# Order of the softmax steps in the differential attention of a hybrid encoder layer

## The chip, the cores and the metric

The kernel runs on one core of a Trainium2 chip. A core has five engines that run side by side, each with its own in-order queue: TensorE (PE: matrix products and transposes into PSUM), VectorE (DVE), ScalarE (ACT), GpSimd (POOL) and SyncE (SP, which issues the DMAs). They wait for one another by semaphores. The metric is the device time of one execution in microseconds (us); lower is better.

## The reference

Two encoder layers over 528 positions (16 learned ones and 512 of the input), width 1024. In each layer one projection feeds four token mixers; their outputs are joined, projected (`w_out`) and added to the residual `h`, and a SwiGLU block follows. The change is in the third mixer, differential attention with 4 heads, each of which has two softmax maps:

```python
def attend(qb):
    p = softmax_probs(qb, k, scale).reshape(b, DIFF_HEADS, 2, qb.shape[1], t)
    amap = p[:, :, 0] - lam_full * p[:, :, 1]
    return jnp.einsum('bhqk,bkhd->bqhd', amap.astype(v.dtype), v)
o = sweep_query_blocks(attend, q)
o = rms_norm(o, out_g) * (1.0 - lambda_init)
```

## The kernel before

The kernel is written for each engine by hand: one function per engine, whose loops give the order of its queue, with semaphore waits between them. Nothing is scheduled by a planner in the stretch of this change. Dense products are made with each operand split in a lead and a rest part (fp32r), three products for each block of 128; ScalarE makes the lead of a weight slot (L1434) and GpSimd the rest (L584, `parts`).

Differential attention is done in 20 **units** (`DIFF_U`), unit u = 5 hp + i: head hp of 4, query tile i of 5 (four of 128 rows, the last of 16). In this text a unit's steps have these names:

- **Scores** (`score_pair`, L1213, TensorE): both score maps of the unit, into PSUM pairs 0 and 1. They may start once the unit before has been exponentiated.
- **Maxima** (`row_max`, L1825 and L1826, VectorE), one for each of the two maps.
- **Exponentials** (`softmax`, L1383, ScalarE), two, into `ebuf`.
- **Inverse sums** (`inverse_sums`, L1840 and L1841, VectorE), then **scaling** of the second map (`scaled_second`, L1394, ScalarE), then the **difference** of the two maps (`difference`, L1847, VectorE) into `mbuf`, which has two buffers.
- **Transposes** (`turn`, L1226 and L1228, TensorE) into one PSUM bank. They wait for the unit's difference and for the rests of the unit before, which free the bank.
- **Leads** (`turned_leads`, L1401, and L1403 for the tail at i = 3, ScalarE) and then **rests** (`turned_rests`, L1855, and L1859 for the tail, VectorE): they take the transposed map out of PSUM as a lead and a rest part.

When the five units of a head are done, **attend** (L800, `pb<-proj_r,v_parts`, 30 products) multiplies the turned map by the values; it waits for the last rests and for the **residual** of the dense group before (`residual`, L1767, VectorE), since both use one PSUM pair. ScalarE then copies the output out and squares it (`out_dif`, L1414 and L1342), TensorE sums the squares (`norm_sum`), ScalarE makes the reciprocal root (`rstd_dif`, L1358 and L1359) and VectorE applies it (`normed`, L1789, **the norm**), on which GpSimd splits the result in lead and rest (`mixed_split`, L610 and L612), followed by the rest part of the next weight slot (L584). Between these steps TensorE does pieces of the output projection (**dense pieces**, `beside`; L800 in layer 0, and L830 to L832 in layer 1): 12, 12, 12, 6 and 6 products in the units of head 0, and none, none, 18, 18 and 12 in the units of each later head in layer 0.

Of the kernel before, what the change touches and what calls it, by code (L numbers as in the profile page):

```python
# [97 lines left out]
DIFF_U = DIFF_H * NT  # L98
N_MAP = MLA_H + DIFF_H
N_EV = NT + 1  # L100
N_ATT_M = MLA_H * NT
# [57 lines left out]
def trunk(nc, x_t, w_stream, w_heads, params, consts, out):  # L159
    ctx = ExitStack()  # L160
    with ctx:
# [67 lines left out]
        def tile_of(buf, k, a=0, b=T, rows_=slice(0, P)):  # L229
            return buf[rows_, k * T + a:k * T + b]  # L230
# [92 lines left out]
        def turn_unit(u):  # L323

            return (u // NT, u % NT) if u < N_ATT_M else (MLA_H + (u - N_ATT_M) // NT, (u - N_ATT_M) % NT)
# [5 lines left out]
        def turned_blocks(tile0, i):  # L331

            a, w = TILES[i]
            n = NT - 1 if i < NT - 1 else NT
            return proj_r[:, tile0 * T:(tile0 + n) * T].rearrange("p (j t) -> p j t", t=T)[:, :, a:a + w]
# [7 lines left out]
        def turned_tail(tile0):  # L343

            return proj_r[0:TILES[-1][1], (tile0 + NT - 1) * T:(tile0 + NT - 1) * T + 512]
# [14 lines left out]
        def dense_part(u):  # L360

            hp, i = u // NT, u % NT
            if hp == 0:
                return ((0, 2), (2, 4), (4, 6), (6, 7), (7, 8))[i]
            return (None, None, (0, 3), (3, 6), (6, 8))[i]
# [430 lines left out]
        def _(pe):  # L796
# [7 lines left out]
            def norm_sum(l, s0, n, p, rows_=slice(0, P), ones="ones"):  # L804

                for k in range(n):
                    pe.wait_ge(sq_ready.sem, sq_ready.at(l, s0 + k + 1))
                    product(p, C(ones, rows_), sq[rows_, (s0 + k) % 2, :], k == 0, k == n - 1).then_inc(sq_used.sem, 1)
# [36 lines left out]
            def beside(l, g, j, operand, chunks):  # L845

                if chunks[j][0] == 0 and chunks[j][1] > 0:
                    pe.wait_ge(evac.sem, evac.at(l, g))
                split_product(l, g, *chunks[j], operand)
# [265 lines left out]
            for l in range(DEPTH):  # L1115
# [89 lines left out]
                def score_pair(u):  # L1205

                    hp, i = u // NT, u % NT
                    pe.wait_ge(p_ready.sem, p_ready.at(l, N_ATT_M + 2 * u))
                    a, w = TILES[i]
                    for b in range(2):  # L1210
                        for m in range(2):
                            r = slice(64 * m, 64 * m + 64)
                            last = nc.tensor.matmul(pb[0:w, 2 * m + b, 0:HALF], tile_of(proj, DQ + hp, a, a + w, r),  # L1213
                                                    tile_of(proj, DK + hp, b * HALF, (b + 1) * HALF, r), start=True, stop=True)
                            if b == 1:
                                last.then_inc(s_ps.sem, 1)
# [40 lines left out]
                for n in range(N_ATT_M):  # L1257
                    hd, i = n // NT, n % NT
# [23 lines left out]
                pe.wait_ge(evac.sem, evac.at(l, G_OUT1 + 3))  # L1282
                norm_sum(l, SQ_A, 4, 3)
                pe.wait_ge(tr_evac.sem, tr_evac.at(l, TR_DV + NT))
                for u in range(DIFF_U):
                    hp, i = u // NT, u % NT
                    if u + 1 < DIFF_U:
                        score_pair(u + 1)
                    if i == 0 and hp:
                        pe.wait_ge(evac.sem, evac.at(l, G_OUT1 + 3 + hp))  # L1290
                        attend(MLA_H + hp - 1)
                    turn(N_ATT_M + u)
                    if i == 1 and hp:
                        pe.wait_ge(o_evac.sem, o_evac.at(l, MLA_H + hp))
                        norm_sum(l, SQ_O + hp - 1, 1, 3)
                    if dense_part(u):
                        pe.wait_ge(rs_ready.sem, rs_ready.at(l, RS_OD + hp))
                        beside(l, G_OUT1 + 3 + hp, 0, mixed_parts, (dense_part(u),))
                pe.wait_ge(evac.sem, evac.at(l, G_OUT2 - 1))
                attend(N_MAP - 1)  # L1300
                beside(l, G_OUT2 - 1, 0, mixed_parts, ((0, KD),))
# [29 lines left out]
        def _(act):  # L1331
# [64 lines left out]
            def turned_leads(l, u):  # L1396

                m, i = turn_unit(u)
                act.wait_ge(t_ps.sem, t_ps.at(l, u + 1))
                act.wait_ge(tails_zero.sem, tails_zero.at(l, 1))  # L1400
                nc.scalar.activation(turned_blocks(PT_LEAD, i), turned_sums(i), ACT.Copy).then_inc(pt_lead.sem, 1)  # L1401
                if i == NT - 2:
                    nc.scalar.activation(turned_tail(PT_LEAD), tail_sums(), ACT.Copy).then_inc(pt_lead.sem, 1)  # L1403
# [151 lines left out]
            for l in range(DEPTH):  # L1555
# [93 lines left out]
                for n in range(N_ATT_M):  # L1649
                    hd, i = n // NT, n % NT  # L1650
# [29 lines left out]
                rsqrt(l, SQ_A + 4, 3, 512, rstd2)  # L1680
                for u in range(DIFF_U):
                    hp, i = u // NT, u % NT
                    if i or hp == 0:
                        turned_leads(l, N_ATT_M + u)
                    if u + 1 < DIFF_U:
                        softmax(l, N_ATT_M + 2 * u + 2)
                        softmax(l, N_ATT_M + 2 * u + 3)
                        scaled_second(l, u + 1)
                    if i == 0 and hp:
                        out_dif(l, hp - 1)  # L1690
                        turned_leads(l, N_ATT_M + u)
                    if i == 0:
                        lead(l, S_OUT1 + 4 + hp)
                    if i == 1 and hp:
                        rstd_dif(l, hp - 1)
# [29 lines left out]
        def _(dve):  # L1725
# [37 lines left out]
            def residual(l, g, k):  # L1763

                dve.wait_ge(w_used.sem, w_used.at(l, slot_end(g)))
                now = of_group(l, g, h[:, k, :])
                nc.vector.tensor_tensor(now, now, group_sum(l, g), ALU.add).then_inc(evac.sem, 1)  # L1767
# [54 lines left out]
            def row_max(l, n):  # L1822
                dve.wait_ge(s_ps.sem, s_ps.at(l, n + 1))
                dve.wait_ge(p_ready.sem, p_ready.at(l, max(n - 1, 0)))
                link(nc.vector.tensor_reduce(rowmax[:, n % 2:n % 2 + 1], pair(n % 2), AX.XY, ALU.max))  # L1825
                nc.vector.tensor_scalar(negmax[:, n % 2:n % 2 + 1], rowmax[:, n % 2:n % 2 + 1], -scale_of(n), None,  # L1826
                                        ALU.mult).then_inc(max_ready.sem, 1)
# [22 lines left out]
            def turned_rests(l, u):  # L1850

                m, i = turn_unit(u)
                e = m * N_EV + i
                dve.wait_ge(pt_lead.sem, pt_lead.at(l, e + 1 + (i == NT - 1)))
                nc.vector.tensor_tensor(turned_blocks(PT_REST, i), turned_sums(i), turned_blocks(PT_LEAD, i).bitcast(FP32),  # L1855
                                        ALU.subtract).then_inc(pt_rest.sem, 1)
                if i == NT - 2:
                    dve.wait_ge(pt_lead.sem, pt_lead.at(l, e + 2))
                    nc.vector.tensor_tensor(turned_tail(PT_REST), tail_sums(), turned_tail(PT_LEAD).bitcast(FP32),  # L1859
                                            ALU.subtract).then_inc(pt_rest.sem, 1)  # L1860
# [223 lines left out]
            for l in range(DEPTH):  # L2084
# [15 lines left out]
                for g in range(G_SSD):  # L2100
# [16 lines left out]
                    if g == MISC + 2:  # L2117
# [4 lines left out]
                        u, ln = ebuf[d24, 0, :], ebuf[d24, 1, :]  # L2122
# [75 lines left out]
                for n in range(N_ATT_M):  # L2198
                    hd, i = n // NT, n % NT
# [18 lines left out]
                for i in range(NT):  # L2218
# [3 lines left out]
                    nc.vector.tensor_tensor(parts_of[:, :, 1, :], pb[0:w, 4 + (TR_DV + i) % 2, 0:512].rearrange("p (h v) -> p h v", h=DIFF_H),  # L2222
                                            parts_of[:, :, 0, :].bitcast(FP32), ALU.subtract).then_inc(tr_evac.sem, 1)
                residual(l, G_OUT1 + 2, 2)
                for u in range(DIFF_U):
                    hp, i = u // NT, u % NT
                    if u + 1 < DIFF_U:
                        row_max(l, N_ATT_M + 2 * u + 2)
                        row_max(l, N_ATT_M + 2 * u + 3)
                    if i or hp == 0:  # L2230
                        turned_rests(l, N_ATT_M + u)
                    if u + 1 < DIFF_U:
                        inverse_sums(l, u + 1)
                        difference(l, u + 1)
                    if i == 0 and hp:
                        turned_rests(l, N_ATT_M + u)
                    if u == 0:
                        dve.wait_ge(rs_ready.sem, rs_ready.at(l, RS_OA + 1))
                        for f in range(4):
                            normed(l, tile_of(mix_f, 12 + f), par_at(l, "mla_out_g", f), count=(f == 3))  # L2240
                    if i == 2 and hp:
                        dve.wait_ge(rs_ready.sem, rs_ready.at(l, RS_OD + hp))
                        normed(l, tile_of(proj, DV + hp - 1), gain_d[:, :])
                    if i == NT - 1:
                        residual(l, G_OUT1 + 3 + hp, 3 + hp)
# [195 lines left out]
```

## Time and profile before

| | |
|---|---|
| median of 3 runs | 2339.93 us (2337.79 to 2340.47) |
| the profiled execution, its own time | 2344.09 us |
| its span, first to last instruction | 2342.3 us |
| busy PE, DVE, ACT, POOL | 2118.8, 1089.6, 854.8, 997.9 us |
| mean granted TensorE clock | 0.972 |
| differential attention, layer 0 (first scores of unit 1 to the last attend) | 620.63 to 735.36 us |
| the same in layer 1 | 1798.08 to 1912.35 us |

TensorE is busy for 90% of the span, so it is the engine that sets the time of the kernel as a whole; but that is a mean over stages, and in the two stretches of the last two lines it is busy for 71% only. The table's last two lines are starts of rows of the trace, which give the place of the stretches. A row of a timeline reads: start, duration, engine, line of the kernel, operation, out<-in, shapes, count; in brackets the idle time of that engine just before, and what ended it.

### The profile page before, as it was taken

The numbers are of one execution on the slowest core, as the hardware profiler recorded it, in microseconds if no ns is written. First come the engines' busy times: TensorE is split into PE (matmuls) and PEld (weight loads), VectorE is DVE, ScalarE is ACT, GpSimd is POOL, SyncE is SP. The second block draws the span as 40 slices with busy tenths as digits, with TensorE's granted clock in tenths as the row PEclk, the third lists the DMA queues.
The fourth block names the chain that finished last, engine by engine and source line by source line (L and its number), as shares of the span: only waits on it lengthen the run. The fifth ranks groups of instructions, "written<-read, shape, count | busy, mean of one in ns | idle before, by whom it ended". The sixth has DMA issues, their size and how long they took to land.

```text
span 2342.3 us, 33441 instructions
## 1 busy us (share of the span) xinstructions
PE 2118.8 (90%) x13634; PEld 1822.7 (78%) x13634; DVE 1089.6 (47%) x1699; ACT 854.8 (36%) x1400; POOL 997.9 (43%) x592
## 2 busy tenths in 40 slices
PE   7999998878778999999989999988777779999999
PEld 7888886556667999999988888865555557888887
DVE  8642354555565644441066322545555657444400
ACT  3322343566554222222223222435665543222221
POOL 4365333664312444444433554336642124444444
PEclk9999999899999999999999999998999899999999
DMA  4211111000001222223322211110000012232333
GB/s 155 64 56 62 47 55 54 10 1 19 19 19 46 83 91 90 91 90 99 99 73 64 64 55 55 46 63 10 1 19 19 19 35 92 91 99 91 98 102 114
DMA packets 40040, 143.85 MB, mean 61 GB/s; under 512 B 4433, under 2 KB 4561, under 8 KB 39761
## 3 DMA queue, kind: packets, MB, share of 16 engines
q1 hardware_dynamic: 39888, 141.72, 18.9%
q8 instruction: 109, 1.79, 0.3%
q14 instruction: 43, 0.34, 0.0%
HBM read 139.60 MB, written 2.10 MB: 60 GB/s over the span
## 4 chain that ended last, share of the span: by engine, by line
PE 71%; DVE 14%; ACT 8%; issue 4%; POOL 1%; DMA 1%; ACTq 0%; SPq 0%; DVEq 0%; POOLq 0%
PE pb L800 44%; PE pb L831 6%; PE pb L830 6%; PE pb L832 6%; ACT ebuf L1383 3%; DVE kh L1779 2%; PE pb L1226 2%; DVE rowmax L1825 1%; ACT ebuf L1394 1%; DVE proj L1761 1%; DVE mbuf L1847 1%; ACT rstd L1358 1%; PE pb L1082 1%; ACT rstd L1359 1%; PE pb L930 1%
## 5 line engine op out<-in xcount | busy, mean ns | idle before, releaser
L584 POOL TENSOR_TENSOR parts<-raw,parts 128x1024 fp32r<-128x1024 f32 x248 | 604.8, 2439 | 844.4 <-ACT parts L1434 844.2
L800 PE MATMUL pb<-mix,parts 128*128 128x264 f32 x4608 | 671.0, 294 | 40.3 <-POOL parts L584 17.1
L800 PEld LDWEIGHTS pb<-mix,parts 128*128 128x128 f32 x4608 | 609.5, 194 | 65.6 <-issue 28.1
L1434 ACT ACTIVATE parts<-raw 128x1024 fp32r<-128x1024 f32 x248 | 262.4, 1058 | 826.7 <-PE pb L800 525.1
L800 PE MATMUL pb<-proj_r,parts 128*128 128x264 f32 x3104 | 429.1, 286 | 0.5 <-POOL parts L584 0.5
L800 PEld LDWEIGHTS pb<-proj_r,parts 128*128 128x128 f32 x3104 | 401.2, 189 | 0.8 <-issue 0.7
L830 PE MATMUL pb<-proj_r,parts 128*128 128x512 f32 x528 | 207.4, 393 | 0.8 <-DVE mbuf L1761 0.8
L832 PE MATMUL pb<-proj_r,parts 128*128 128x512 f32 x528 | 207.7, 393 | 0.0
L831 PE MATMUL pb<-proj_r,parts 128*128 128x512 f32 x496 | 198.0, 399 | 0.0
L1767 DVE TENSOR_TENSOR h<-h,pb 128x528 f32<-128x528 f32 (+1 forms) x48 | 33.3, 694 | 272.7 <-PE pb L800 139.1
L1383 ACT ACTIVATE ebuf<-pb,negmax 128x528 f32<-128x528 f32 x160 | 110.9, 696 | 56.0 <-DVE negmax L1826 55.5
L1761 DVE TENSOR_TENSOR mbuf<-pb,rstd 128x528 f32<-128x528 f32 (+1 forms) x44 | 30.8, 700 | 214.8 <-PE pb L800 110.5
L1761 DVE TENSOR_TENSOR proj<-pb,rstd 128x528 f32<-128x528 f32 x80 | 56.5, 706 | 156.3 <-PE pb L800 143.3
L1825 DVE TENSOR_REDUCE rowmax<-pb 128x1 f32<-128x528 f32 x160 | 112.6, 704 | 31.5 <-PE pb L800 20.4
L800 PE MATMUL pb<-sq,con 128*128 128x264 f32 (+1 forms) x328 | 91.2, 409 | 31.4 <-ACT sq L1629 22.1
L830 PEld LDWEIGHTS pb<-proj_r,parts 128*128 128x128 f32 x528 | 99.2, 188 | 24.9 <-DVE mbuf L1761 1.2
L832 PEld LDWEIGHTS pb<-proj_r,parts 128*128 128x128 f32 x528 | 99.3, 188 | 22.4
L2272 DVE CAST proj_r<-ebuf 128x528 fp32r<-128x528 f32 x44 | 110.9, 2521 | 1.5
L831 PEld LDWEIGHTS pb<-proj_r,parts 128*128 128x128 f32 x496 | 94.7, 191 | 20.8
L800 PE MATMUL pb<-proj_r,v_parts 128*128 128x264 f32 x560 | 81.2, 305 | 25.2 <-ACT rstd L1359 16.2
L800 PEld LDWEIGHTS pb<-proj_r,v_parts 128*128 128x128 f32 x560 | 76.1, 206 | 35.3 <-ACT rstd L1359 21.2
L800 PE MATMUL pb<-proj,w_head 128*112 128x264 f32 (+1 forms) x320 | 85.2, 417 | 15.8 <-DMA w_head<-w_heads 9.8
(273 smaller groups left out, 2877.7 us busy)
## 6 DMA issues: line engine op xcount, KB each, us to landing
raw<-w_stream SPq DMA_DIRECT2D x250, 512.0 KB, 3.5
w_head<-w_heads SPq DMA_DIRECT2D x8, 512.0 KB, 4.8
h<-x_t SPq DMA_DIRECT2D x8, 264.0 KB, 6.6
out_t<-h SPq DMA_DIRECT2D x8, 256.0 KB, 4.9
con<-consts SPq DMA_DIRECT2D x1, 1652.5 KB, 10.3
par<-params SPq DMA_DIRECT2D x1, 340.0 KB, 4.4
con<-consts SPq DMA_DIRECT2D x1, 128.0 KB, 6.8
```

Of the source, the lines that this page charges most:

```text
L584: nc.gpsimd.tensor_tensor(parts[:, n % PARTS, 1, :], w, parts[:, n % PARTS, 0, :].bitcast(FP32), ALU.subtract).then_inc(split.sem, 1)
L800: last = nc.tensor.matmul(pb[rows_, 2 * p + a, 0:HALF], lhs_t, rhs[:, a * HALF:(a + 1) * HALF], start=start, stop=stop)
L830: nc.tensor.matmul(o, w_lead, lead[:, kept(l, g)], start=(k == 0), stop=False)
L831: nc.tensor.matmul(o, w_lead, rest[:, kept(l, g)], start=False, stop=False)
L832: last = nc.tensor.matmul(o, w_rest, lead[:, kept(l, g)], start=False, stop=(k == k_all - 1))
L1226: nc.tensor.transpose(pb[:, TURN, j * step:j * step + P], src[:, j * P:(j + 1) * P], C("ident"))
L1383: nc.scalar.activation(halves(ebuf[:, b, :]), pair(b), ACT.Exp, scale=scale_of(n), bias=negmax[:, b:b + 1], accum_out=sums[:, n % 4:n % 4 ...
L1434: nc.scalar.activation(parts[:, n % PARTS, 0, :], raw[:, r % RAW, :], ACT.Copy).then_inc(lead_ready.sem, 1)
L1761: nc.vector.tensor_tensor(of_group(l, g, dst), group_sum(l, g), of_group(l, g, rstd[:, :]), ALU.mult).then_inc(evac.sem, 1)
L1779: ins = nc.vector.scalar_tensor_tensor(out=acc[:, a:b], in0=src[:, a + s:b + s], scalar=par_at(l, "conv_w", f * TAPS + mid + s), in1=acc[: ...
L1825: link(nc.vector.tensor_reduce(rowmax[:, n % 2:n % 2 + 1], pair(n % 2), AX.XY, ALU.max))
L2272: link(nc.vector.tensor_copy(lead, prod))
```

## The change

In the loop over the units the steps are written in another order, on three engines. On ScalarE the leads of a unit now always stand behind the next unit's exponentials and scaling, as they did before at i = 0 only. On VectorE the rests now always stand behind the next unit's difference, and the maxima are made for the unit after the next, behind the rests. On TensorE the scores of unit u+2 are written at the end of unit u instead of at the start of unit u+1.

```diff
@@ TensorE
+                score_pair(1)
                 for u in range(DIFF_U):
                     hp, i = u // NT, u % NT
-                    if u + 1 < DIFF_U:
-                        score_pair(u + 1)
                     if i == 0 and hp:
...
                         beside(l, G_OUT1 + 3 + hp, 0, mixed_parts, (dense_part(u),))
+                    if u + 2 < DIFF_U:
+                        score_pair(u + 2)
@@ ScalarE
                     hp, i = u // NT, u % NT
-                    if i or hp == 0:
-                        turned_leads(l, N_ATT_M + u)
                     if u + 1 < DIFF_U:
                         softmax(l, N_ATT_M + 2 * u + 2)
                         softmax(l, N_ATT_M + 2 * u + 3)
                         scaled_second(l, u + 1)
                     if i == 0 and hp:
                         out_dif(l, hp - 1)
-                        turned_leads(l, N_ATT_M + u)
+                    turned_leads(l, N_ATT_M + u)
@@ VectorE
+                row_max(l, N_ATT_M + 2)
+                row_max(l, N_ATT_M + 3)
                 for u in range(DIFF_U):
                     hp, i = u // NT, u % NT
                     if u + 1 < DIFF_U:
-                        row_max(l, N_ATT_M + 2 * u + 2)
-                        row_max(l, N_ATT_M + 2 * u + 3)
-                    if i or hp == 0:
-                        turned_rests(l, N_ATT_M + u)
-                    if u + 1 < DIFF_U:
                         inverse_sums(l, u + 1)
                         difference(l, u + 1)
-                    if i == 0 and hp:
-                        turned_rests(l, N_ATT_M + u)
+                    turned_rests(l, N_ATT_M + u)
+                    if u + 2 < DIFF_U:
+                        row_max(l, N_ATT_M + 2 * u + 4)
+                        row_max(l, N_ATT_M + 2 * u + 5)
                     if u == 0:
...
```

The queue of TensorE has the same 3507 rows in the same order in both kernels: the scores of unit u+2 at the end of one turn of the loop and at the start of the next are the same place. So the change is one of ScalarE and VectorE alone. All lines behind the change stand one or two lower in the new kernel.

ScalarE before, head 1, from the leads of unit 6 on:

```order
L1401 ACTIVATE proj_r<-pb 128x4x128
L1383 ACTIVATE ebuf,sums<-pb,negmax 128x528 x2
L1394 ACTIVATE ebuf<-ebuf,rsum 128x528
L1358 ACTIVATE rstd<-pb,eps 128x528
L1359 ACTIVATE rstd<-rstd 128x528
L1401 ACTIVATE proj_r<-pb 128x4x128
L1383 ACTIVATE ebuf,sums<-pb,negmax 128x528 x2
L1394 ACTIVATE ebuf<-ebuf,rsum 128x528
```

and now, from the exponentials of unit 7 on:

```order
L1384 ACTIVATE ebuf,sums<-pb,negmax 128x528 x2
L1395 ACTIVATE ebuf<-ebuf,rsum 128x528
L1402 ACTIVATE proj_r<-pb 128x4x128
L1359 ACTIVATE rstd<-pb,eps 128x528
L1360 ACTIVATE rstd<-rstd 128x528
L1384 ACTIVATE ebuf,sums<-pb,negmax 128x528 x2
L1395 ACTIVATE ebuf<-ebuf,rsum 128x528
L1402 ACTIVATE proj_r<-pb 128x4x128
```

The leads (L1401, now L1402) have moved from ahead of the next unit's exponentials to behind its scaling.

VectorE before, from the maxima of unit 8 through the norm (L1789) to the maxima of unit 9:

```order
L1825 TENSOR_REDUCE rowmax<-pb 128x1
L1826 TENSOR_SCALAR negmax<-rowmax 128x1
L1855 TENSOR_TENSOR proj_r<-pb,proj_r 128x4x128
L1840 RECIPROCAL rsum<-sums 128x2
L1841 TENSOR_TENSOR rsum<-rsum,neg_lam 128x1
L1847 SCALAR_TENSOR_TENSOR mbuf<-ebuf,rsum 128x528
L1789 SCALAR_TENSOR_TENSOR proj<-proj,gain_d,rstd 128x528
L1825 TENSOR_REDUCE rowmax<-pb 128x1
L1826 TENSOR_SCALAR negmax<-rowmax 128x1
```

and now, from the inverse sums of unit 8 on:

```order
L1839 RECIPROCAL rsum<-sums 128x2
L1840 TENSOR_TENSOR rsum<-rsum,neg_lam 128x1
L1846 SCALAR_TENSOR_TENSOR mbuf<-ebuf,rsum 128x528
L1854 TENSOR_TENSOR proj_r<-pb,proj_r 128x4x128
L1824 TENSOR_REDUCE rowmax<-pb 128x1
L1825 TENSOR_SCALAR negmax<-rowmax 128x1
L1824 TENSOR_REDUCE rowmax<-pb 128x1
L1825 TENSOR_SCALAR negmax<-rowmax 128x1
L1788 SCALAR_TENSOR_TENSOR proj<-proj,gain_d,rstd 128x528
```

The rests (L1855, now L1854) stand behind the difference, the maxima behind the rests, and the norm behind the maxima.

VectorE before, at the end of a head, from the last unit's rests (L1855, 128x5x16) over the residual (L1767) to the maxima of the next head's second unit:

```order
L1855 TENSOR_TENSOR proj_r<-pb,proj_r 128x5x16
L1840 RECIPROCAL rsum<-sums 128x2
L1841 TENSOR_TENSOR rsum<-rsum,neg_lam 128x1
L1847 SCALAR_TENSOR_TENSOR mbuf<-ebuf,rsum 128x528
L1767 TENSOR_TENSOR h<-h,pb 128x528
L1825 TENSOR_REDUCE rowmax<-pb 128x1
L1826 TENSOR_SCALAR negmax<-rowmax 128x1
```

and now:

```order
L1846 SCALAR_TENSOR_TENSOR mbuf<-ebuf,rsum 128x528
L1854 TENSOR_TENSOR proj_r<-pb,proj_r 128x5x16
L1824 TENSOR_REDUCE rowmax<-pb 128x1
L1825 TENSOR_SCALAR negmax<-rowmax 128x1
L1824 TENSOR_REDUCE rowmax<-pb 128x1
L1825 TENSOR_SCALAR negmax<-rowmax 128x1
L1766 TENSOR_TENSOR h<-h,pb 128x528
```

The residual, for which attend waits, now has the last rests and two maxima ahead of it as well as the difference.

## Rows read from the trace of the kernel before

**Rows 1.** Busy time in head 0 of layer 0, by engine (windows view)
```profile
core 0: us, PE busy (x) PEld busy (x) DVE busy (x) ACT busy (x) POOL busy (x), PEclk, DMA share, GB/s
620.63:649.93 29.30, 17.74 (x122) 13.56 (x121) 20.62 (x47) 16.08 (x34) 13.66 (x9) 0.94 0.07 19
```
**Rows 2.** Waits of TensorE, 616 to 740 us: us in total, times, longest
```profile
PE pb L1226 <- DVE mbuf L1847: 16.5, 12, 3.6
PE pb L1213 <- ACT ebuf L1383: 10.4, 9, 2.9
```
**Rows 3.** Timeline of TensorE, layer 0, head 1: transposes of units 6, 7, 9, scores
```profile
658.07 0.63 PE L1226 MATMUL pb<-con,mbuf 128*128 128x128 f32 x4 [1.04 <-DVE proj_r L1855]
662.82 0.65 PE L1226 MATMUL pb<-con,mbuf 128*128 128x128 f32 x4 [0.81 <-DVE mbuf L1847]
665.71 1.07 PE L1213 MATMUL pb<-proj 64*16 64x264 f32 x8
674.16 1.03 PE L1226 MATMUL pb<-con,mbuf 128*128 128x128 f32 x4 [2.13 <-DVE mbuf L1847]
```
**Rows 4.** Timeline of VectorE, one unit: maxima, inverse sum, difference, rests, maxima
```profile
649.80 0.70 DVE L1825 TENSOR_REDUCE rowmax<-pb 128x1 f32<-128x528 f32 x1
652.36 0.17 DVE L1840 RECIPROCAL rsum<-sums 128x2 f32<-128x2 f32 x1 [0.86 <-ACT ebuf L1383]
653.52 0.77 DVE L1847 SCALAR_TENSOR_TENSOR mbuf<-ebuf,rsum 128x528 f32<-128x528 f32 x1 [0.80 <-ACT ebuf L1394]
657.23 0.69 DVE L1855 TENSOR_TENSOR proj_r<-pb,proj_r 128x512 fp32r<-128x512 f32 x1 [2.94 <-ACT proj_r L1401]
657.84 0.70 DVE L1825 TENSOR_REDUCE rowmax<-pb 128x1 f32<-128x528 f32 x1
659.47 0.69 DVE L1855 TENSOR_TENSOR proj_r<-pb,proj_r 128x512 fp32r<-128x512 f32 x1
666.78 0.77 DVE L1847 SCALAR_TENSOR_TENSOR mbuf<-ebuf,rsum 128x528 f32<-128x528 f32 x1 [0.80 <-ACT ebuf L1394]
```
**Rows 5.** Timeline of VectorE: rests and tail at i = 3, the next inverse sum
```profile
669.77 0.68 DVE L1855 TENSOR_TENSOR proj_r<-pb,proj_r 128x512 fp32r<-128x512 f32 x1
670.96 0.14 DVE L1840 RECIPROCAL rsum<-sums 128x2 f32<-128x2 f32 x1
```
**Rows 6.** End of head 0, layer 0: last transposes, last rests, residual, attend
```profile
644.90 0.65 PE L1226 MATMUL pb<-con,mbuf 128*128 128x128 f32 x4 [0.81 <-DVE mbuf L1847]
646.39 0.23 DVE L1855 TENSOR_TENSOR proj_r<-pb,proj_r 128x80 fp32r<-128x80 f32 x1
649.18 0.70 DVE L1767 TENSOR_TENSOR h<-h,pb 128x528 f32<-128x528 f32 x1
649.93 5.46 PE L800 MATMUL pb<-proj_r,v_parts 128*128 128x264 f32 x30 [1.42 <-DVE h L1767]
```
**Rows 7.** VectorE and GpSimd side by side, from the norm of head 0
```profile
667.46 0.76 DVE L1789 SCALAR_TENSOR_TENSOR proj<-proj,gain_d,rstd 128x528 f32<-128x528 f32 x1
668.31 1.53 POOL L610 TENSOR_SCALAR mix<-proj 128x528 fp32r<-128x528 f32 x1 [25.07 <-DVE proj L1789]
669.93 1.31 POOL L612 TENSOR_TENSOR proj_r<-proj,mix 128x528 fp32r<-128x528 f32 x1
671.20 2.35 POOL L584 TENSOR_TENSOR parts<-raw,parts 128x1024 fp32r<-128x1024 f32 x1
672.10 2.01 DVE L1847 SCALAR_TENSOR_TENSOR mbuf<-ebuf,rsum 128x528 f32<-128x528 f32 x1 [0.80 <-ACT ebuf L1394]
```
**Rows 8.** Head 0, layer 0: first maxima, the four norms, GpSimd's run
```profile
621.82 0.71 DVE L1825 TENSOR_REDUCE rowmax<-pb 128x1 f32<-128x528 f32 x1 [5.18 <-PE pb L1213]
626.37 2.80 DVE L1789 SCALAR_TENSOR_TENSOR mix_f<-mix_f,par,rstd 128x528 f32<-128x528 f32 x4
629.25 1.53 POOL L610 TENSOR_SCALAR mix<-mix_f 128x528 fp32r<-128x528 f32 x1 [20.67 <-DVE mix_f L1789]
640.90 2.35 POOL L584 TENSOR_TENSOR parts<-raw,parts 128x1024 fp32r<-128x1024 f32 x1
```

## The prediction

> **What bounds the kernel now.** I read the page first for the share of each engine, then the busy times of the two stretches in which differential attention runs, then TensorE's waits there, and last the timelines, since the change is an order of instructions. TensorE sets the time of the kernel, but in head 0 of this stage it is busy for 17.74 of 29.30 us, and no other engine for more than 20.62 [rows 1]. So no engine is full: the stage is a chain that goes from engine to engine. TensorE's waits say which. Of the 114.7 us of the stretch in layer 0, 16.5 are waits of the transposes for the difference of the maps, and 10.4 are waits of the scores for the exponentials [rows 2]. Both point at the softmax of the next unit.
>
> In a plain unit before, the chain closes through the transposes: transposes of unit u, its leads on ScalarE, the exponentials of u+1 behind them, inverse sum, scaling, difference of u+1, transposes of u+1. One turn is 4.75 us (658.07 to 662.82) [rows 3]. In it TensorE has its own work, transposes and 18 dense products, 2.89 us from 662.82 to 665.71, and 1.07 of scores [rows 3]. Together that is 4.0, so at most some 0.8 us of a turn is open to a better order.
>
> **The change, part by part.** *TensorE.* Its queue has the same rows in the same order, so this edit costs and gives nothing. "Two units ahead" was already so. SP's queue and GpSimd's are untouched, and the order of the weight leads on ScalarE too.
>
> *The new chain.* ScalarE now exponentiates u+1 ahead of the leads of u, so the transposes and leads leave the chain. But VectorE has its whole work for a unit in one row, and it makes the maxima of u+2 only behind the rests of u. What ScalarE may exponentiate next hangs on those maxima. The new turn is therefore: maxima of u+1, exponentials, inverse sum, scaling, difference of u+1, rests of u, maxima of u+2. Each step has a row. From the first of the two maxima to the inverse sum, 649.80 to 652.36, 2.56; from there to the difference, 653.52, 1.16; from a difference to the next VectorE instruction, 666.78 to 667.46, 0.68 [rows 4, 7]; from rests to maxima, 657.23 to 657.84, 0.61 [rows 4]. The sum is 5.01 us. The leads are not what is late in it: the scaling and then the leads end before VectorE has got through the difference. The scores are there in time at full clock: they start 2.89 behind the transposes, which follow the rests by 0.84 (657.23 to 658.07) [rows 3, 4], so the maxima find them some 0.7 us early. Transposes come one per turn, so a plain unit goes from 4.75 to 5.01: it takes 0.26 more. The cover that the old order had (the maxima stood under the transposes and leads) is what is given up.
>
> *Units 6 to 9 of each later head.* Before, from the transposes of unit 6 to those of unit 9 it is 16.09 us (658.07 to 674.16) [rows 3]: two plain turns, and a third of 6.56 with a tail and a stall in it. The stall is the difference that took 2.01 instead of 0.77, 1.24 us, while GpSimd's subtraction of 671.20 to 673.55 ran [rows 4, 7]. Now: three turns of 5.01 are 15.03, since the tail of unit 8 falls behind the rests for which unit 9's transposes wait. Whether the stall remains is a matter of place. The norm now stands behind the maxima of unit 9, so it starts 2.56 - 1.63 = 0.93 us before the inverse sum (two maxima are 1.63, 657.84 to 659.47 [rows 4]) and the difference 2.09 behind its start. GpSimd's first subtraction begins 2.47 behind the norm's start (667.46 to 669.93) and its second ends 6.09 behind (to 673.55) [rows 7]. The difference gets in 0.4 us ahead of the first, and the next unit's two-input instructions come at some 6.7, behind the second. So I take the stall as gone: 15.03 - 16.09 = -1.06 for each of three heads.
>
> The Trainium skill, "SBUF — State Buffer", section "🔬 SBUF: two separate sides", says that VectorE and GpSimd share a port pair as an exclusive lock, held for a whole instruction, and that a VectorE instruction with two SBUF inputs is of the kind that needs it. The trace agrees: the difference ran on past the end of GpSimd's subtraction, and the rests, which read PSUM and took 0.68 under the other subtraction at 669.77 [rows 5, 7], did not. By that rule a shift of 0.4 us turns the gain into a loss, which is rival B.
>
> *The end of a head.* Attend waits for the residual, and the residual now has more ahead of it. Before, from the last unit's transposes to attend is 5.03 us (644.90 to 649.93) [rows 6]. Now, from the rests of unit 3 on: tail 1.19 (669.77 to 670.96) [rows 5], maxima and exponentials of the next unit 2.56, inverse sum to difference 1.16, difference 0.68, last rests 0.23 (646.39) [rows 6], two more maxima 1.63, residual to attend 0.75 (649.18 to 649.93) [rows 6]. That is 8.20 from the rests of unit 3, and the transposes of unit 4 stand 0.84 behind those, so 7.36: +2.33. Behind attend the order is that of before (leads at i = 0 were already behind the scaling), so nothing changes up to unit 6. The last head has no maxima left to put ahead of the residual: 0.
>
> *Head 0.* From its first maxima (621.82 [rows 8]) to the rests of unit 0 is 2.56 + 1.16 + 0.68 = 4.40, the next maxima follow 0.61 behind and end at 628.46. The four norms (2.80 [rows 8]) now stand there, over the exponentials of unit 2, to 631.26; the rests of unit 1 follow at 631.26 + 1.16 + 0.68 = 633.10. Two turns more bring the rests of unit 3 to 643.1, and 8.20 more attend to 651.3, against 649.93: +1.4. Stalls come on top. GpSimd's run of four splits and a weight part started 2.88 behind the norms (629.25) and ended at 643.25 [rows 8]; it shifts by the 2.1 us of the norms, and the new instants of the inverse sums and the difference fall in up to three of its subtractions, by my walk 3.0 us in all. Since fractions of a microsecond decide each, I take 2.0, between none and 3.0. Head 0: +3.4.
>
> **The sum.** One layer: head 0 +3.4; heads 1 and 2 each -1.06 + 2.33 = +1.27, together +2.5; head 3 -1.06. That is +4.9, and both layers have the same order: +9.8 us. The profiled execution (2344.09: the span of 2342.3 and 1.8 around it) would go to 2353.9; it stood 4.2 over the median of the runs, so against the median of 2339.93 I say 2349.7.
>
> The bounds: with no stall in head 0, 2.9 a layer, +5.8 and 2345.7. With all of them, +11.8 and 2351.7. TensorE's lowered clock is a second term. Unit 9's transposes took 1.03 instead of 0.65, and attend 5.46 [rows 3, 6]; in such a stretch the scores come later than the 0.7 us that the new chain has in hand. From double durations (2.89 more) this would cost up to 2 us each; two or three in a layer, if they fall so, are +4 to +8 for both layers. I leave it out of the centre and keep it in the range.
>
> **The rivals.** *A. The intended gain.* If VectorE kept pace with TensorE, a unit would take 4.0 us. Units 6 to 9 would go to 12, -4.1 for three heads, -1.5 in head 0, +2.3 for three heads' ends: -7 a layer, 2326. It decides where VectorE's serial row is under 4.0; the rows add up to 5.01. A weaker form (the end of a head cheaper, fewer lowered-clock stretches) stays between 2326 and 2335. Against it: attend's place behind the residual is in the order itself. For it: the waits for the difference, 16.5 us [rows 2], are real, and they are what the edit goes for. 12 in 100.
>
> *B. The stall moves and grows.* If the difference of unit 9 is 0.4 us later than worked out, it meets both subtractions in a row and waits 3.3 us, in three heads and two layers: +20, so 2369. If only half of them fall so, 2359. The margin is small, but it is made of VectorE's own row and a fixed lag of GpSimd, which move together. 12 in 100, with 3 of them at the full price.
>
> *C. It cancels.* If the residual's delay is half covered (its dense piece ends late anyway at a lowered clock, as in the head of rows 3) and head 0 has no new stalls, what units 6 to 9 give, -6.4 in all, meets half of the ends, +4.7, and head 0's +2.8: +1.1, so 2341. 13 in 100.
>
> **How the numbers follow.** My forecast has 63 in 100, with its own range 2345 to 2357. From no change one can tell 0.2%, that is 4.7 us. Slower is my case and B, 75 in 100; the same C, 13; faster A, 12. The range reaches down into C and up into B: 2339 to 2361.
>
> **What would show it.** In the profile after: transposes of plain units 5.0 us apart, with the wait before them named for the rests (L1854) and no longer for the difference; ScalarE's leads with no wait; maxima 0.6 behind the rests. From the last transposes of a head to attend 7.4 us, with the residual as releaser; in the last head 3 to 5. Unit 9's difference 0.77 long, and long ones, if any, in head 0. Heads 1 and 2 each 1.3 longer, head 3 one shorter. I am wrong if a plain unit is under 4.75, if attend is not held by the residual, or if the difference of unit 9 still runs for 2 us or more.

## The result and the profile after

The changed kernel is slower: median 2358.49 us (2355.15 to 2360.26, 4 runs) against 2340.2 us for the kernel before (4 runs), ratio 1.0072, 95% interval 1.0054 to 1.0090. The profiled execution took 2360.26 us, its span 2358.4: 16.1 more than before. All of it lies in differential attention. From the first scores of unit 1 to the last attend, layer 0 went from 114.7 to 121.5 us and layer 1 from 114.3 to 124.0, +16.5 together.

The two largest waits of TensorE in layer 0 of the changed kernel (waiting line, releaser, us in total, times, longest):

```profile
PE pb L1226 <- DVE proj_r L1854: 25.3, 16, 3.7
PE pb L800 <- DVE h L1766: 10.9, 5, 3.2
```

The transposes no longer wait for the difference, as in [rows 2], but for the rests; and attend's wait for the residual is now the second largest. Both were foretold; how long each is the timelines show. VectorE in head 1 of the changed kernel, one plain unit, then unit 9's product of the inverse sum with `neg_lam` (L1840) and its difference (start, duration, line, operation):

```profile
668.63 0.70 DVE L1824 TENSOR_REDUCE rowmax<-pb 128x1 f32<-128x528 f32 x1
671.20 0.17 DVE L1839 RECIPROCAL rsum<-sums 128x2 f32<-128x2 f32 x1 [0.86 <-ACT ebuf L1384]
672.36 0.77 DVE L1846 SCALAR_TENSOR_TENSOR mbuf<-ebuf,rsum 128x528 f32<-128x528 f32 x1 [0.80 <-ACT ebuf L1395]
673.04 0.68 DVE L1854 TENSOR_TENSOR proj_r<-pb,proj_r 128x512 fp32r<-128x512 f32 x1
673.64 0.69 DVE L1824 TENSOR_REDUCE rowmax<-pb 128x1 f32<-128x528 f32 x1
676.41 0.34 DVE L1840 TENSOR_TENSOR rsum<-rsum,neg_lam 128x1 f32<-128x1 f32 x1
677.55 0.77 DVE L1846 SCALAR_TENSOR_TENSOR mbuf<-ebuf,rsum 128x528 f32<-128x528 f32 x1 [0.80 <-ACT ebuf L1395]
```

From maxima to maxima it is 5.01 us (668.63 to 673.64), and the steps are those of [rows 4] within 0.01: 2.57, 1.16, 0.68, 0.60. The difference of unit 9 takes 0.77 instead of the 2.01 of [rows 7]. What TensorE does in the same head (transposes of units 6 to 9, then attend):

```profile
663.85 0.63 PE L1226 MATMUL pb<-con,mbuf 128*128 128x128 f32 x4 [1.04 <-DVE proj_r L1854]
668.86 0.63 PE L1226 MATMUL pb<-con,mbuf 128*128 128x128 f32 x4 [1.49 <-DVE proj_r L1854]
673.87 0.63 PE L1226 MATMUL pb<-con,mbuf 128*128 128x128 f32 x4 [1.08 <-DVE proj_r L1854]
679.07 0.63 PE L1226 MATMUL pb<-con,mbuf 128*128 128x128 f32 x4 [1.20 <-DVE proj_r L1854]
686.36 5.45 PE L800 MATMUL pb<-proj_r,v_parts 128*128 128x264 f32 x30 [3.19 <-DVE h L1766]
```

Units 6 to 9 take 15.22 us (16.09 in [rows 3]), and the last transposes to attend 7.29 (5.03 in head 0 before, [rows 6]). New in this head is the duration of attend itself, 5.45 us. In the kernel before it was:

```profile
679.68 3.92 PE L800 MATMUL pb<-proj_r,v_parts 128*128 128x264 f32 x30 [0.64 <-DVE h L1767]
```

The windows view of the changed kernel, for the stretch ahead of attend and for attend itself (columns as in [rows 1]):

```profile
682.01:686.36 4.35, 1.16 (x9) 0.69 (x9) 3.39 (x9) 2.28 (x6) 0.00 (x0) 1.00 0.39 121
686.36:691.65 5.29, 5.29 (x31) 5.29 (x31) 1.09 (x3) 0.90 (x3) 0.00 (x0) 0.68 0.00 0
```

TensorE works for 1.16 of 4.35 us, then runs attend at a granted clock of 0.68 on average, a mix of 1.2 and 2.4 GHz; in the 15.7 us behind it the granted clock is 1.00 again. Before, of the six attends of heads 0 to 2 in both layers, two took about 5.5 us and four 3.9, 26.6 us in all. Now all six take 5.3 to 6.6, 34.3 us in all: +7.7. (The attends of the last head, which lie behind the end of the two stretches, took 5.6 and 5.9 us before and take 3.9 and 6.1 now.)

### The profile page after: what moved, and what is told of

It is laid out like the page before. It is cut to its first block, busy times and chain, and to the rows that moved or that the text cites. A ratio compares the mean times of both kernels' runs of the same rounds, so it can differ in the third digit from the quotient of the medians.

```text
span 2358.4 us, 33441 instructions
## 1 busy us (share of the span) xinstructions
PE 2121.2 (90%) x13634; PEld 1824.6 (77%) x13634; DVE 1086.5 (46%) x1699; ACT 858.0 (36%) x1400; POOL 1001.5 (42%) x592
## 4 chain that ended last, share of the span: by engine, by line
PE 70%; DVE 16%; ACT 8%; issue 4%; POOL 1%; DMA 1%; SPq 0%; ACTq 0%; DVEq 0%; POOLq 0%
PE pb L800 44%; PE pb L830 6%; PE pb L831 6%; PE pb L832 6%; DVE rowmax L1824 3%; ACT ebuf L1384 2%; DVE kh L1778 2%; DVE proj_r L1854 1%; PE pb L1226 1%; DVE proj L1760 1%; ACT ebuf L1395 1%; ACT rstd L1359 1%; PE pb L1082 1%; ACT rstd L1360 1%; PE pb L930 1%
## 5 line engine op out<-in xcount | busy, mean ns | idle before, releaser
L800 PE MATMUL pb<-proj_r,v_parts 128*128 128x264 f32 x560 | 87.4, 321 | 37.4 <-DVE h L1766 21.2
L800 PEld LDWEIGHTS pb<-proj_r,v_parts 128*128 128x128 f32 x560 | 82.3, 222 | 47.4 <-DVE h L1766 25.6
L610 POOL TENSOR_SCALAR mix<-proj 128x528 fp32r<-128x528 f32 x22 | 34.7, 1579 | 160.8 <-DVE proj L1788 160.1
```

The lines of the kernel that those rows point to most:

```text
L610: nc.gpsimd.tensor_scalar(lead, mixed_source(k), 1.0, None, ALU.mult).then_inc(mixed_lead.sem, 1)
L800: last = nc.tensor.matmul(pb[rows_, 2 * p + a, 0:HALF], lhs_t, rhs[:, a * HALF:(a + 1) * HALF], start=start, stop=stop)
```

## The experiments

Each ratio is that of a kernel to the kernel before, measured side by side on one chip. Where two of these ratios are compared with each other, both intervals count.

**The residual ahead of the maxima (e1_res_first).**

```diff
                     turned_rests(l, N_ATT_M + u)
+                    if i == NT - 1:
+                        residual(l, G_OUT1 + 3 + hp, 3 + hp)
                     if u + 2 < DIFF_U:
                         row_max(l, N_ATT_M + 2 * u + 4)
                         row_max(l, N_ATT_M + 2 * u + 5)
...
-                    if i == NT - 1:
-                        residual(l, G_OUT1 + 3 + hp, 3 + hp)
```

> The changed kernel, with the residual of the dense group put ahead of the two maxima at the end of a head, and nothing else. Theory (the row of VectorE sets the pace): from the last transposes of a head to attend it takes the 1.63 us of two maxima less, in three heads of two layers, -9.8 us, so about 2348.7; plain units stay at 5.01 us. Rival (TensorE's lowered clock in attend is brought on by the idle time ahead of it, 3.2 us in the changed kernel): the idle time falls to 1.6 us and attend goes back from 5.4 to 3.9 us in most heads, up to -9 more, so 2340. Rival (the residual is held by its dense piece and not by the maxima): no change, 2358.

Ratio 0.9999 (0.9987 to 1.0011): the whole loss is gone, 17 us of it. The row of VectorE alone asked for 9.8 of them, the reading with the clock for up to 9 more. In the trace of this kernel, the last transposes of head 1 and the attend behind them:

```profile
675.18 0.63 PE L1226 MATMUL pb<-con,mbuf 128*128 128x128 f32 x4 [1.18 <-DVE proj_r L1854]
680.85 3.89 PE L800 MATMUL pb<-proj_r,v_parts 128*128 128x264 f32 x30 [1.56 <-DVE h L1766]
```

From transposes to attend it is 5.67 instead of 7.29 us: the 1.63 of two maxima, 9.7 us in six places. Attend's wait is 1.56 instead of 3.19, and five of the six attends run at 3.9 us, 25.4 us in all in place of 34.3. So the residual's place is confirmed as its own term, and the rest, some 7 us, comes with the clock. The third reading, that the dense piece holds the residual, falls.

**VectorE's order alone (e2_vector_only).** ScalarE's part of the diff taken back. (ScalarE's part alone can't be run: leads behind the next scaling, with rests ahead of the next inverse sums, wait for each other.)

```diff
+                    if i or hp == 0:
+                        turned_leads(l, N_ATT_M + u)
                     if u + 1 < DIFF_U:
                         softmax(l, N_ATT_M + 2 * u + 2)
...
                     if i == 0 and hp:
                         out_dif(l, hp - 1)
-                    turned_leads(l, N_ATT_M + u)
+                        turned_leads(l, N_ATT_M + u)
```

> VectorE's order of the changed kernel with ScalarE's order of the kernel before (leads ahead of the next exponentials). Theory (one chain through all engines): transposes, leads 0.80, exponentials 0.50 + 0.67, inverse sum 0.83, difference 1.16, rests 0.68, transposes 0.84 make a turn of 5.5 us, against 4.75 before and 5.01 in the changed kernel, and the end of a head is as long as in the changed kernel: some 13 us a layer over the kernel before, about 2367. Rival (ScalarE's new order is what costs): it comes out at the time of the kernel before or up to 5 us over it.

Ratio 1.0154 (1.0129 to 1.0179), +36 us where 27 were expected. A turn is 5.45 us, as the chain says:

```profile
698.61 0.63 PE L1226 MATMUL pb<-con,mbuf 128*128 128x128 f32 x4 [1.04 <-DVE proj_r L1856]
704.07 0.63 PE L1226 MATMUL pb<-con,mbuf 128*128 128x128 f32 x4 [1.50 <-DVE proj_r L1856]
```

So VectorE's order is what costs; ScalarE's part of the change gives some of it back (5.45 to 5.01 a turn). Of the 9 us over my expectation 6.8 can be put down to attends at the lowered clock, by one trace: its six take 33.4 us in place of 26.6.

**Work in place of idling (e3_fill, e9_before_fill).** In the changed kernel five extra products, in the kernel before two:

```diff
                     if i == 0 and hp:
+                        pe.wait_ge(pt_rest.sem, pt_rest.at(l, (MLA_H + hp - 1) * N_EV + NT))
+                        for _ in range(5):
+                            nc.tensor.matmul(pb[:, TAIL, 0:HALF], C("ones"), C("cos_d")[:, 0:HALF], start=True, stop=True)
                         pe.wait_ge(evac.sem, evac.at(l, G_OUT1 + 3 + hp))
```

> The changed kernel, with five extra products (128x264, into the unused tail bank, results never read) on TensorE ahead of attend's wait in heads 1 to 3, so that it works through 2.6 of the 3.2 us for which it stood idle. Theory clock (the idle time ahead of attend brings the lowered clock): attend goes from 5.4 back to 3.9 us in most heads, -6 to -9 us in all, 2350 to 2352. Rival (the clock is lowered by what was done long before, or at fixed times): attend's mean length stays at 5.4 or grows, and the time stays within 2 us of 2358.

> The kernel before with two extra products of 128x264 on TensorE ahead of attend's wait in heads 1 to 3 (results never read), 1.0 of the 1.4 us that it idled there. Theory clock: of the three attends a layer that this reaches, one took 5.5 us in the kernel before; it goes to 3.9, -3 us in two layers, ratio 0.997 to 0.9985. The filled forms of both kernels (this one, and the changed kernel with five extra products, ratio 1.0027) then differ by what the order of the steps costs without the clock's share: by the prediction's terms 9.8 us, 0.42% of the time. Rival (the clock's share in the change is small, the chain costs all 17 us): this run comes out 15 us or more under the filled changed kernel, at 0.996 or less.

The changed kernel with the extra products: ratio 1.0027 (1.0016 to 1.0038), so useless work took 10 us off (6 to 15 with both intervals; 6 to 9 were expected). Its windows for the same two stretches as above:

```profile
686.11:690.46 4.35, 3.58 (x19) 2.51 (x19) 3.39 (x9) 2.28 (x6) 0.00 (x0) 1.00 0.37 121
690.46:694.21 3.75, 3.75 (x31) 3.75 (x31) 1.09 (x3) 0.90 (x3) 0.00 (x0) 1.00 0.02 4
```

The stretch ahead of attend is as long as before, 4.35 us, and attend runs at 2.4 GHz throughout. All six attends are at 3.9 to 4.0, 10.7 us less than in the changed kernel. That attend runs slowly because TensorE does little ahead of it is shown: only that was changed, and all 18 attends behind extra products in the three kernels that have them (e3, e9, e7) took 3.9 to 4.0 us. The Trainium skill, "TensorE: Matmul & The Clock Gate", section "🔬 Part 1: The HAM clock gate (the "warmup" mystery)", calls the low rate the default which activity releases; by that rule the trace agrees, 0.68 becoming 1.00.

The kernel before with extra products came out at 0.9997 (0.9987 to 1.0007). Its six attends took 23.7 us instead of 26.6, but no gain can be measured, where 0.997 to 0.9985 was expected; in its trace four groups of transposes in the later heads still took 1.04 to 1.12 us instead of 0.66, so the lowered clock was not gone from them. The filled forms of both kernels differ by 0.30%, some 7 us; with both intervals 3.5 to 10.5. That is what the order costs without the clock's share in attend, and my 9.8 lies in it; the rival of 15 us or more does not. The agreement is partly luck. In the two traces the stretches differ by 10.0 us, but 9.4 of it is in head 0, where the prediction has 6.8 (the five products outlast attend's shorter wait there, by 1.2 us in both layers), and 0.6 in heads 1 to 3, where it has 3.0.

**GpSimd's two-input instructions (e5_one_input, e6_before_one_input).** In both kernels those of this stage become one-input instructions, which copy the source. The subtraction is left out, so these two kernels don't compute the reference; only their times are used.

```diff
-                nc.gpsimd.tensor_tensor(parts[:, n % PARTS, 1, :], w, parts[:, n % PARTS, 0, :].bitcast(FP32),
-                                        ALU.subtract).then_inc(split.sem, 1)
+                if S_OUT1 + 4 <= s < S_OUT2:
+                    nc.gpsimd.tensor_scalar(parts[:, n % PARTS, 1, :], w, 1.0, None, ALU.mult).then_inc(split.sem, 1)
+                else:
+                    nc.gpsimd.tensor_tensor(parts[:, n % PARTS, 1, :], w, parts[:, n % PARTS, 0, :].bitcast(FP32),
+                                            ALU.subtract).then_inc(split.sem, 1)
...
-                nc.gpsimd.tensor_tensor(other, mixed_source(k), lead.bitcast(FP32), ALU.subtract).then_inc(mixed.sem, 1)
+                if k < KD:
+                    nc.gpsimd.tensor_tensor(other, mixed_source(k), lead.bitcast(FP32), ALU.subtract).then_inc(mixed.sem, 1)
+                else:
+                    nc.gpsimd.tensor_scalar(other, mixed_source(k), 1.0, None, ALU.mult).then_inc(mixed.sem, 1)
```

> The changed kernel, in which GpSimd makes the rest parts of the mixed rows 8 to 14 and of the weight slots of the stretch (four a layer) by one-input instructions (a copy of the source in place of source minus lead, so these rest parts are not the reference's). Theory (VectorE's two-input instructions wait behind GpSimd's two-input subtractions): the waits of head 0 in the changed kernel's trace, 0.45 + 0.68 + 0.81 + 1.28 = 3.2 us, and 0.18 in each later head go, 3.7 us a layer, -7.5 us: ratio to the kernel before about 1.004, 2351 us. The difference and the product with neg_lam then always take 0.77 and 0.16 us. Rival (they are long for another reason, such as PSUM or a DMA): their lengths and the time stay, 2358.

> The kernel before, with the same one-input instructions on GpSimd (the same rest parts left wrong). Theory: the 1.24 us stall in each of three heads and 0.7 us in head 0 go, 4.4 to 5.2 us a layer, -9 to -10 us, 2331. With the run on the changed kernel this prices the term 'the stall is gone': the difference between both kernels without any stall should be 11 to 12 us worse for the change where lowered clocks are alike. Rival: no change, 2340.

The kernel before gains as expected, 0.9959 (0.9943 to 0.9975), 9.6 us. The changed kernel comes to 1.0064 (1.0041 to 1.0087): 2 us under its own ratio, which the intervals don't separate from none. The 3.7 us a layer were expected to go entirely. By the trace 2.6 of them went in layer 0 and 2.0 in layer 1, and head 0 became 1.8 to 1.9 us shorter in each. What stays shows in the changed kernel, where VectorE's product at 676.41 (above, 0.34 long where it is 0.16 elsewhere) meets GpSimd's one-input instruction:

```profile
676.11 1.53 POOL L610 TENSOR_SCALAR mix<-proj 128x528 fp32r<-128x528 f32 x1 [29.17 <-DVE proj L1788]
677.73 1.75 POOL L612 TENSOR_TENSOR proj_r<-proj,mix 128x528 fp32r<-128x528 f32 x1
```

The product ends at 676.75, 0.64 us behind GpSimd's start. In the traces of the changed kernel, e4, e5, e6 and e8 there are 38 such products, which begin up to 0.31 us behind the start of a one-input instruction of this shape, and every one ends 0.63 to 0.66 behind that start, while a difference that begins later, 0.85 us behind such a start at 639.64 in the changed kernel, keeps its 0.77 us. So a one-input instruction on GpSimd also holds VectorE's two-input product up, for its first 0.6 of 1.5 us; the prediction took the hold to be for a whole instruction and of two-input ones only. That is part of why the expectation for this run was too high, and it is the 0.18 us by which the third turn (5.20) is over 5.01. The second row shows how near rival B was: unit 9's difference began at 677.55, 0.18 us ahead of the first subtraction, where the prediction counted on 0.4.

**A third order (e4_between), with the norm in its old place (e8_between_norm2), and filled (e7_between_fill).** If VectorE's row sets the pace, an order that puts its rests into a wait that it has anyway should be faster:

```diff
@@ ScalarE
                         softmax(l, N_ATT_M + 2 * u + 3)
+                    if i or hp == 0:
+                        turned_leads(l, N_ATT_M + u)
+                    if u + 1 < DIFF_U:
                         scaled_second(l, u + 1)
                     if i == 0 and hp:
                         out_dif(l, hp - 1)
-                    turned_leads(l, N_ATT_M + u)
+                        turned_leads(l, N_ATT_M + u)
...
@@ VectorE
                         inverse_sums(l, u + 1)
+                    if i or hp == 0:
+                        turned_rests(l, N_ATT_M + u)
+                    if u + 1 < DIFF_U:
                         difference(l, u + 1)
-                    turned_rests(l, N_ATT_M + u)
+                    if i == 0 and hp:
+                        turned_rests(l, N_ATT_M + u)
+                    if i == NT - 1:
+                        residual(l, G_OUT1 + 3 + hp, 3 + hp)
...
-                    if i == 2 and hp:
+                    if i == 3 and hp:
                         dve.wait_ge(rs_ready.sem, rs_ready.at(l, RS_OD + hp))
                         normed(l, tile_of(proj, DV + hp - 1), gain_d[:, :])
-                    if i == NT - 1:
-                        residual(l, G_OUT1 + 3 + hp, 3 + hp)
```

At i = 0 of the later heads ScalarE's leads stay behind `out_dif`. The residual stands ahead of the maxima here too, as in e1.

> A third order. ScalarE: exponentials of u+1, leads of u, scaling of u+1. VectorE: inverse sums of u+1, rests of u, difference of u+1, then the residual, then the maxima of u+2; the norm one unit later (i = 3). At i = 0 as in the changed kernel. Theory (the row of VectorE sets the pace): the rests stand under the scaling instead of behind the difference, so a turn is maxima 1.63, exponentials and inverse sum 0.93 and 0.83, leads and rests under the scaling, 1.35 to the difference, 0.68: about 4.5 us against 4.75 before; the end of a head is shorter by 1.6 us than in the changed kernel; unit 9's difference escapes GpSimd's subtractions. Together some 7 to 9 us a layer under the kernel before: 2322 to 2327. Rival (VectorE's order makes no difference, only ScalarE's leads do): about 2340.

> The third order with the norm left at i = 2 as in both kernels. Theory (GpSimd's subtractions start 2.5 us behind the norm): the shorter turn of 4.4 us puts the second inverse sum or difference behind the norm into the second subtraction again, 1 to 1.5 us in three heads of two layers, so 2330 to 2334, between the third order (2324.7) and the kernel before. Rival (the place of the norm is of no account): 2325.

> The third order (exponentials, leads, scaling) with three extra products of 128x264 on TensorE ahead of attend's wait in heads 1 to 3, results never read; 1.5 of the 1.6 us that it idled there. Theory clock (work in place of idling keeps the clock up): the four attends that took 5.45 us go back to 3.92, -6 us, 2319. Rival (the clock is lowered by something else): the count of slow attends stays, time 2325, or a little more where the extra products end late.

The third order gives 0.9925 (0.9904 to 0.9947), as expected, 17.6 us under the kernel before and 34 under the changed one. By e1 half of the 34 belongs to the residual's place. VectorE in the third order:

```profile
662.36 0.70 DVE L1827 TENSOR_REDUCE rowmax<-pb 128x1 f32<-128x528 f32 x1
664.93 0.17 DVE L1842 RECIPROCAL rsum<-sums 128x2 f32<-128x2 f32 x1 [0.86 <-ACT ebuf L1384]
665.41 0.69 DVE L1857 TENSOR_TENSOR proj_r<-pb,proj_r 128x512 fp32r<-128x512 f32 x1
666.09 0.77 DVE L1849 SCALAR_TENSOR_TENSOR mbuf<-ebuf,rsum 128x528 f32<-128x528 f32 x1
666.77 0.70 DVE L1827 TENSOR_REDUCE rowmax<-pb 128x1 f32<-128x528 f32 x1
```

From inverse sum to difference it is still 1.16 us, but now the rests stand in it, where VectorE waited for the scaling. The turn is 4.41 us. The norm's old place costs nothing that can be measured: 0.9923 (0.9901 to 0.9944), although unit 9's difference then takes 1.68 us. The stall came as expected, the loss of 5 us or more did not. By the traces four of six attends ran slow with the new place and one with the old, which gives back most of what the stall takes; that is an account after the fact. With three extra products the third order is the fastest kernel of this study, 0.9878 (0.9857 to 0.9899), median 2317.05 us; all its attends take 3.9 to 4.0. The gain over the third order is 11 us, 4 to 18 with both intervals; the slow attends had cost 6 there by my count, which lies in it. The windows view of its head 2:

```profile
676.12:701.58 25.46, 21.26 (x153) 16.90 (x153) 18.19 (x44) 17.34 (x36) 5.65 (x4) 1.00 0.06 22
```

A head is 25.46 us long there, at a granted clock of 1.00; in the changed kernel it was 30.6.

## Why the prediction was right, and where it was not

The direction and its mechanism were right: 2349.7 was forecast in 2339 to 2361, and 2358.5 was measured. The size was half: +9.8 against +18.3 by the medians, +16.5 in the two stretches. The measured time is over the 2345 to 2357 of my own case; it lies in the whole range only because that was stretched for rival B, whose 2359 was met without its mechanism. That is luck. Of the signs that I named, the turn, the releasers, 7.4 us to attend and the length of unit 9's difference came as said, the lengths of the heads did not.

- *TensorE's part changes nothing.* Right by its queue, which is the same.
- *A turn of 5.01 us in place of 4.75.* Right to 0.01. e2 (5.45) and e4 (4.41) confirm the chain from both sides, each order having its own sum.
- *Units 6 to 9: -1.06.* Measured 15.22 against 16.09, -0.87, in the head of the rows. The stall is gone, as foretold; the 0.18 us is GpSimd's one-input instruction, which I had taken to be harmless. Over all six heads it is -1.08 on average, since two of them took 17.42 and 16.66 before (one with a stall of 2.00 us instead of 1.24, both with transposes at a lowered clock). Rival B, the stall that grows, did not occur, but 0.18 us of margin was all that was left.
- *The end of a head: +2.33.* Measured 7.29 - 5.03 = +2.26; over all six heads 7.3 against 5.0 to 5.6, +2.02 on average. e1 shows that most of it, 1.62, is the residual's place. The last head's end, set at 0, became 0.6 us shorter.
- *Head 0: +3.4.* Measured +4.6 and +3.9. The stalls that I walked through to 3.0 us and then set at 2.0 all occurred. In layer 0 three under subtractions make 0.68 + 0.81 + 1.28 = 2.8 us, and a fourth, under a one-input instruction, adds 0.45. The walk should have been trusted.
- *"TensorE's lowered clock is a second term ... I leave it out of the centre and keep it in the range."* This term failed. I priced it through late scores (+4 to +8, where two or three a layer at up to 2 us make up to 8 to 12) and gave it 0 in the sum. In fact it sits in attend: six attends took 34.3 us in place of 26.6, +7.7, and e3 took 10.7 off them by filling the wait ahead. Every step that I had made longer was a wait of TensorE, and at the end of a head it grew from at most 1.4 us to 2.4 to 3.2. I had the row that shows the price, attend at 5.46 [rows 6], and counted only late scores from it.
- *The terms together.* By the traces the 9.8 us became 16.5 so: +1.7 in head 0, -1.3 at the ends of heads 1 and 2, -1.2 at those of the last heads, and +7.7 in attend. The misses other than attend's nearly offset each other.
- *Rivals A and C.* A fell on VectorE's sum; what it hoped for is what e4 then did, by making that sum 4.41. C asked for a half covered residual, and it was not covered at all.

Heads 1 to 3 changed by +0.9, +1.6, -0.3 in layer 0 and +1.3, +3.5, +1.1 in layer 1. Two layers with one order differ mostly by what the clock did, so only their sum is held against the prediction.

## What to carry to other kernels

Where no engine is full, write down for each engine the row of its steps in one turn, with the steps of others between, and take the largest sum: a step that is moved off one chain lands in some engine's row, and here it was VectorE's. Work that nothing waits for yet (here two maxima) belongs behind the instruction that the busiest engine waits for (the residual), and other work into a wait that the row has anyway (the rests under the scaling). A longer wait of TensorE has a second price, in the clock of what follows.

## What the runs showed of the hardware that I had not expected

- The same 30 products take 3.9 us or 5.3 to 6.6. Where the windows above show both, the granted clock is 1.00 or 0.68 on average. In the changed kernel, e2 and e5, all 13 attends with a wait of 2.9 to 3.2 us ahead were slow, and four of five with 2.4 to 2.8. With waits of 2.1 us in e4 and e8 none of four was, with 1.4 to 1.6 us both occurred (3.89 behind 1.56 in e1, 5.45 behind 1.60 in e4), and in the last heads both occurred behind 0.8 us (3.91 and 6.09 in the changed kernel). So the wait just ahead does not decide by itself; what else does stays open.
- Extra products with unused results, put into a wait, made two of three kernels faster: by 10 us (e3 against the changed kernel) and by 11 us (e7 against e4), with the intervals given above. In the kernel before they made no measurable difference (0.9987 to 1.0007).
- A one-input GpSimd instruction of 1.53 us held VectorE's two-input product up for its first 0.63 us, 38 times out of 38. A longer one (128x1024, 2.77 us) held it until 1.05 us behind its start, twice in e6.
